# Differential attention: probabilities times values as 24 split products of 512 columns a head

## What is computed

```python
def one_block(args):                      # one block of 128 queries
    qi, pi = args
    sc = jnp.einsum('bhcqd,bhckd->bhcqk', qi, k_t).astype(jnp.float32) * scale
    ...
    p = jax.nn.softmax(sc, axis=-1)
    p_diff = p[:, :, 0] - lam * p[:, :, 1]
    return jnp.einsum('bhqk,bhkd->bhqd', p_diff.astype(v_t.dtype), v_t)
...
o = diff_attend(q, k, v, pos, lam)
o = rms_norm(o, subln_g) * (1.0 - lam_init)
return x + (o.reshape(b, s, B_WIDTH) * jax.nn.silu(gate)) @ w_out
```

## Time and profile before

| | |
|---|---|
| median of 3 runs | 3137.69 us (3137.46 to 3138.93) |
| the profiled execution: its time, its span | 3139.25 us, 3137.5 us |
| TensorE busy | 3095.8 us, 99% of the span |
| VectorE, ScalarE, GpSimd busy | 1523.7, 808.1, 2066.2 us |
| chain of work that ended last | TensorE 91%, VectorE 5% |
| TensorE clock granted, mean | 0.996 of full speed |

### The profile page before, as it was taken

The page is one execution under the profiler, slowest core; times in us unless marked ns, Lnnn a source line. Parts: engine busy times, 40 slices in busy tenths (PEclk is TensorE's granted clock), DMA queues, the critical chain, the costliest instruction groups (busy, mean ns, idle before and its releaser), DMA issues.

```text
span 3137.5 us, 59104 instructions
## 1 busy us (share of the span) xinstructions
PE 3095.8 (99%) x19614; PEld 2481.1 (79%) x19614; DVE 1523.7 (49%) x2996; ACT 808.1 (26%) x1560; POOL 2066.2 (66%) x3468
## 2 busy tenths in 40 slices
PE   8999999999999999999999999999999999999999
PEld 6777777788888787788778878888888888888777
DVE  3565555566565765611566773144234324433600
ACT  2333332243333203200355551021112112211300
POOL 7555555488787695887733456886666766666575
PEclk9999999999999999999999999999999999999999
DMA  5222221232222232233211112332222222222142
GB/s 160 62 62 62 62 61 57 62 92 80 74 80 78 70 94 78 80 94 94 74 41 33 47 40 81 94 98 81 81 74 74 80 80 74 74 81 79 54 127 87
DMA packets 461252, 239.59 MB, mean 76 GB/s; under 512 B 27917, under 2 KB 456392, under 8 KB 461128
## 3 DMA queue, kind: packets, MB, share of 16 engines
q1 hardware_dynamic: 457148, 232.14, 25.5%
q10 hardware_dynamic: 3980, 5.63, 0.5%
HBM read 233.52 MB, written 4.19 MB: 76 GB/s over the span
## 4 chain that ended last, share of the span: by engine, by line
PE 91%; DVE 5%; issue 2%; ACT 1%; DMA 0%; DVEq 0%; POOL 0%; SPq 0%; ACTq 0%; PEldq 0%; POOLq 0%
PE proj L346 25%; PE proj L347 24%; PE proj L348 24%; PE work L2598 2%; PE work L2180 2%; PE work L2173 1%; PE work L726 1%; PE work L1289 1%; PE work L346 1%; PE work L348 1%; PE work L347 1%; PE work L740 1%; PE work L1544 1%; PE work L1530 1%; DVE lat_sq L1835 0%
## 5 line engine op out<-in xcount | busy, mean ns | idle before, releaser
L318 POOL TENSOR_SCALAR w_hi<-raw_weights 128x256 fp32r<-128x256 f32 x1728 | 742.8, 456 | 1037.5 <-DMA raw_weights<-w_in 350.8
L322 POOL TENSOR_TENSOR w_lo<-raw_weights,w_hi 128x256 fp32r<-128x256 f32 x1728 | 1331.4, 801 | 0.0
L346 PE MATMUL proj<-x_hi,w_hi 128*128 128x512 f32 x2976 | 1217.7, 409 | 7.6 <-POOL w_lo L322 3.0
L347 PE MATMUL proj<-x_lo,w_hi 128*128 128x512 f32 x2976 | 1176.9, 395 | 0.0
L348 PE MATMUL proj<-x_hi,w_lo 128*128 128x512 f32 x2976 | 1176.2, 395 | 0.0
L346 PEld LDWEIGHTS proj<-x_hi,w_hi 128*128 128x128 f32 x2976 | 559.7, 188 | 152.8 <-issue 20.8
L348 PEld LDWEIGHTS proj<-x_hi,w_lo 128*128 128x128 f32 x2976 | 558.8, 188 | 136.6
L347 PEld LDWEIGHTS proj<-x_lo,w_hi 128*128 128x128 f32 x2976 | 560.3, 188 | 118.7 <-issue 2.2
L346 PE MATMUL proj<-o_hi,w_hi 128*128 128x512 f32 x256 | 103.5, 404 | 3.6 <-DVE o_lo L1175 3.2
L347 PE MATMUL proj<-o_lo,w_hi 128*128 128x512 f32 x256 | 102.0, 398 | 0.0
L348 PE MATMUL proj<-o_hi,w_lo 128*128 128x512 f32 x256 | 101.8, 398 | 0.0
(11 more groups left out here) (491 smaller groups left out, 3922.9 us busy)
## 6 DMA issues: line engine op xcount, KB each, us to landing
raw_weights<-w_in SPq DMA_DIRECT2D x260, 256.0 KB, 3.2
raw_weights<-b_w_in SPq DMA_DIRECT2D x256, 256.0 KB, 3.1
raw_weights<-a_w_in SPq DMA_DIRECT2D x100, 256.0 KB, 3.2
raw_weights<-w_out SPq DMA_DIRECT2D x64, 256.0 KB, 3.0
raw_weights<-a_w_out SPq DMA_DIRECT2D x64, 256.0 KB, 3.0
raw_weights<-b_w_out SPq DMA_DIRECT2D x64, 256.0 KB, 3.0
raw_weights<-a_w_kv_up SPq DMA_DIRECT2D x32, 256.0 KB, 2.8
mix<-x SPq DMA_DIRECT2D x4, 1024.0 KB, 8.5
```

What stands on the lines that cost most here:

```text
L318: pool.tensor_scalar(part(hi_v, s, q), part(raw_v, s, q), 1.0, 1.0, ALU.mult, ALU.mult).then_inc(hi_done, 1)
L322: pool.tensor_tensor(part(lo_v, s, q), part(raw_v, s, q), part(hi_v, s, q).bitcast(F32), ALU.subtract).then_inc(w_split, 1)
L346: pe.matmul(out, w_h, a_h, start=start, stop=False)
L347: pe.matmul(out, w_h, a_l, start=False, stop=False)
```

## The change

The product V is made once a head, for all four query blocks together, in the split form: for each half x of the value channels, four calls of `multiply` over the key blocks c, with 512 columns of queries: 2 x 4 x 3 = 24 matmuls. For this:

- the transposed probabilities of all blocks are kept, as high part (pT on ScalarE writes `d_pt_hi`) and low part, for which VectorE gets a new instruction for each block, `pl`: the transposed block in `work[2]` less its high part; the values get a low part too (`vl0`, `vl1`, VectorE);
- the room for them is taken from blocks 6 to 15 of `mix`: at the start of the stage ScalarE's queue stores these 10 blocks (2.62 MB) to `h_kept` in DRAM, and loads them back behind the last head; ScalarE and VectorE wait for the store before their first head, and VectorE waits for the load before tile 4 of the last product;
- `dpipe` has five steps instead of six; the 6 steps of fill now stand at every k, so also in front of the last transposes; V stands behind them, with 2 steps in front and 4 behind. In all there are 52 steps of fill a head instead of 50 (48 instead of 46 in the last head), and as many fewer behind it;
- T of block k-1 now waits for `pl` of block k-2, where it waited for pT of it; V waits for the last `pl`;
- ScalarE's copies `o` go: it squares V's output from PSUM directly, and VectorE multiplies it into the gates from PSUM (`og` comes before the sums; the final step is one multiplication for each half);
- in the last head VectorE cuts blocks 8 to 13 of `mix2` in pairs, behind the `pl` of blocks 1, 2 and 3 (`behind_block`).

```diff
@@ -2466,7 +2468,14 @@
         d_p = a11.over("diff_probs", d_gt_at, SEQ)
-        d_pt = a11.over("diff_probs_keys", d_gt_at + 4 * SEQ, SEQ)
+        KEPT = range(6, KB)
+        kept_at = o_start + 4 * SEQ * KEPT[0]
+        d_pt_hi, d_pt_lo = (tokens(a11.over(f"diff_probs_keys_{x}", kept_at + 4 * TB * SEQ * n, TB * SEQ, F32R)[:, :], SEQ)
+                            for n, x in enumerate(("hi", "lo")))
+        d_vt_lo = a11.over("diff_v_tok_lo", kept_at + 8 * TB * SEQ, 2 * SEQ, F32R)
+        h_kept = nc.dram_tensor("h_kept", (P, len(KEPT) * SEQ), F32).ap()
+        h_stored = sem("h_stored")
+        h_back = sem("h_back")
         d_small = a11.take("diff_small", 16 * 5)
@@ -2479,7 +2488,7 @@
         d_col = a11.take("diff_pos_col", 2 * TB)
-        dpipe = range(TB + 2)
+        dpipe = range(TB + 1)
 
@@ -2491,11 +2500,13 @@
+        DI_DVE = steps("diff_dve", "ms " + RSQRT + " nsl lq0 lq1 vl0 vl1 gate0 k0 k1 lk0 lk1 gate1 " +
+                       " ".join((f"rec{k - 1} rl{k - 1} pb{k - 1} p{k - 1} " if k else "") +
+                                (f"sca{k} mxa{k} nba{k} scb{k} mxb{k} nbb{k} " if k < TB else "") +
+                                (f"pl{k - 1}" if k else "") for k in range(TB + 1)) +
+                       " og0 oadd og1 oms " + tagged("o_") + " o0 o1")
@@ -2573,40 +2584,39 @@
                         if k == 0:
-                            need(DI_ACT, f"vt{c}")
+                            need(DI_DVE, f"vl{c}")
                             need(DI_DVE, f"lk{c}")
...
                                  True, True).then_inc(DI_PE.mark(f"S{x}{k}"), 1)
-                    yield 3
+                yield 3
                 if 1 <= k <= TB:
...
                     if k >= 2:
-                        need(DI_ACT, f"pT{k - 2}")
+                        need(DI_DVE, f"pl{k - 2}")
                     for c in range(TB):
...
                     yield 1
-                if k >= 2:
-                    need(DI_ACT, f"pT{k - 2}")
-                    if k >= 3:
-                        need(DI_ACT, f"o{k - 3}")
-                    for x in range(2):
-                        for c in range(TB):
-                            mm = pe.matmul(work[3][:, x * P:(x + 1) * P], d_vt[:, 256 * c + x * P:256 * c + (x + 1) * P],
-                                           d_pt[:, c * P:(c + 1) * P], start=(c == 0), stop=(c == TB - 1))
-                    mm.then_inc(DI_PE.mark(f"V{k - 2}"), 1)
-                    yield 1
             yield 1
-            need(DI_DVE, "oadd1")
-            token_sums(pe, work[2], d_sq[0], lambda b: b).then_inc(DI_PE.mark("osum"), 1)
+            need(DI_DVE, f"pl{TB - 1}")
+            for x in range(2):
+                for c in range(TB):
+                    vs = slice(256 * c + x * P, 256 * c + (x + 1) * P)
+                    mm = multiply(pe, work[3 - x], d_vt_hi[:, vs], d_vt_lo[:, vs], d_pt_hi[:, c], d_pt_lo[:, c],
+                                  c == 0, c == TB - 1)
+                mm.then_inc(DI_PE.mark(f"V{x}"), 1)
+            yield 2
+            need(DI_DVE, "oadd")
+            token_sums(pe, work[0], d_sq[0], lambda b: b).then_inc(DI_PE.mark("osum"), 1)
             yield behind_sums
             need(DI_DVE, "o_out_")
-            token_values(pe, work[3], d_small[:, 68:72]).then_inc(DI_PE.mark("oinv"), 1)
+            token_values(pe, work[1], d_small[:, 68:72]).then_inc(DI_PE.mark("oinv"), 1)
 
         def diff_act(act):
+            act.dma_start(h_kept, mix[:, KEPT[0] * SEQ:]).then_inc(h_stored, 16)
             pos = io["positions_2"]
@@ -2619,6 +2629,7 @@
             act.wait_ge(DP_DVE.sem, DP_DVE.after())
+            act.wait_ge(h_stored, 16)
             with act.Fori(0, B_HEADS - 1) as h:
@@ -2627,6 +2638,7 @@
             diff_heads_act(act, B_HEADS - 1, split_first, lambda k: out_split_act(act, OUT3, range(2 * k + 6, 2 * k + 8)))
+            act.dma_start(mix[:, KEPT[0] * SEQ:], h_kept).then_inc(h_back, 16)
             stage_end(act, 8, [(DI_ACT.sem, DI_ACT.after(B_HEADS)), (tile_free, T_DIFF + 8 * B_HEADS)])
@@ -2639,7 +2651,7 @@
                 need(DI_PE, f"vt{x}")
-                act.activation(tokens(d_vt[:, :], 256)[:, :, x * P:(x + 1) * P], tokens(work[x][:, :], P), ACT.Copy)\
+                act.activation(tokens(d_vt_hi[:, :], 256)[:, :, x * P:(x + 1) * P], tokens(work[x][:, :], P), ACT.Copy)\
                    .then_inc(DI_ACT.mark(f"vt{x}"), 1)
@@ -2667,19 +2679,11 @@
                     need(DI_PE, f"T{k - 1}")
-                    if k >= 2:
-                        need(DI_PE, f"V{k - 2}")
-                    act.activation(d_pt[:, :], work[2][:, :], ACT.Copy).then_inc(DI_ACT.mark(f"pT{k - 1}"), 1)
-                if k >= 2:
-                    need(DI_PE, f"V{k - 2}")
-                    act.activation(tokens(d_v[:, :], SEQ)[:, :, (k - 2) * P:(k - 1) * P], tokens(work[3][:, 0:256], P),
-                                   ACT.Copy).then_inc(DI_ACT.mark(f"o{k - 2}"), 1)
-                    if k in (3, TB + 1):
-                        x = k // TB
-                        by_half = lambda v: tokens(v, SEQ)[:, :, x * 2 * P:(x + 1) * 2 * P]
-                        act.wait_ge(DI_ACT.sem, DI_ACT.so_far(p))
-                        act.activation(by_half(d_sqs[:, 0:2 * SEQ]), by_half(d_v[:, :]), ACT.Square)\
-                           .then_inc(DI_ACT.mark(f"osq{x}"), 1)
+                    act.activation(d_pt_hi[:, :, (k - 1) * P:k * P], tokens(work[2][:, :], P), ACT.Copy)\
+                       .then_inc(DI_ACT.mark(f"pT{k - 1}"), 1)
+            for x in range(2):
+                need(DI_PE, f"V{x}")
+                act.activation(d_sq[x][:, :], work[3 - x][:, :], ACT.Square).then_inc(DI_ACT.mark(f"osq{x}"), 1)
 
@@ -2716,13 +2720,14 @@
             dve.wait_ge(NB_ACT.sem, NB_ACT.done("rinv"))
+            dve.wait_ge(h_stored, 16)
             with dve.Fori(0, B_HEADS - 1) as h:
...
             diff_heads_dve(dve, B_HEADS - 1, lambda: out_split_dve(dve, OUT3, FIRST),
-                           lambda: out_split_dve(dve, OUT3, range(*AHEAD3[0])))
+                           lambda k: out_split_dve(dve, OUT3, range(2 * k + 4, 2 * k + 6) if k >= 2 else ()))
             stage_end(dve, 8, [(DI_DVE.sem, DI_DVE.after(B_HEADS))])
 
-        def diff_heads_dve(dve, p, before_scores=lambda: None, behind_scores=lambda: None):
+        def diff_heads_dve(dve, p, before_scores=lambda: None, behind_block=lambda k: None):
             need = lambda steps, name: dve.wait_ge(steps.sem, steps.done(name, p))
@@ -2758,6 +2763,11 @@
                 low(c, dq_lo, d_q, dq_hi, "q")
+            for x in range(2):
+                need(DI_ACT, f"vt{x}")
+                by_block = lambda v: tokens(v[:, :], 256)[:, :, x * P:(x + 1) * P]
+                done(dve.tensor_tensor(by_block(d_vt_lo), tokens(work[x][:, :], P), by_block(d_vt_hi).bitcast(F32),
+                                       ALU.subtract), f"vl{x}")
             take_gate(0)
@@ -2795,21 +2805,29 @@
 
-            behind_scores()
-            for x in range(2):
-                half = slice(x * 2 * P, (x + 1) * 2 * P)
-                need(DI_ACT, f"osq{x}")
-                done(dve.tensor_tensor(d_sq[0][:, half], d_sq[0][:, half], d_sq[1][:, half], ALU.add), f"oadd{x}")
+                if k >= 1:
+                    need(DI_ACT, f"pT{k - 1}")
+                    ks = slice((k - 1) * P, k * P)
+                    done(dve.tensor_tensor(d_pt_lo[:, :, ks], tokens(work[2][:, :], P), d_pt_hi[:, :, ks].bitcast(F32),
+                                           ALU.subtract), f"pl{k - 1}")
+                behind_block(k)
+
+            def weigh(x):
+                done(dve.scalar_tensor_tensor(gate(x), gate(x), sub_gain[:, x:x + 1], work[3 - x][:, :],
+                                              ALU.mult, ALU.mult), f"og{x}")
+
+            need(DI_ACT, "osq0")
+            weigh(0)
+            need(DI_ACT, "osq1")
+            done(dve.tensor_tensor(d_sq[0][:, :], d_sq[0][:, :], d_sq[1][:, :], ALU.add), "oadd")
+            weigh(1)
             need(DI_PE, "osum")
             chain()
-            done(dve.tensor_scalar(work[2][:, 16:20], work[2][:, 0:4], 1.0 / B_V, EPS, ALU.mult, ALU.add), "oms")
-            rsqrt(dve, DI_DVE, p, work[2][:, 16:24], d_small[:, 64:68], d_small[:, 72:76], d_small[:, 68:72], "o_")
+            done(dve.tensor_scalar(work[0][:, 16:20], work[0][:, 0:4], 1.0 / B_V, EPS, ALU.mult, ALU.add), "oms")
+            rsqrt(dve, DI_DVE, p, work[0][:, 16:24], d_small[:, 64:68], d_small[:, 72:76], d_small[:, 68:72], "o_")
             need(DI_PE, "oinv")
             for x in range(2):
-                done(dve.scalar_tensor_tensor(gate(x), gate(x), sub_gain[:, x:x + 1], work[3][:, :],
-                                              ALU.mult, ALU.mult), f"og{x}")
-                chain()
-                done(dve.tensor_tensor(gate(x), gate(x), d_v[:, x * SEQ:(x + 1) * SEQ], ALU.mult), f"o{x}")
```

(17 more changed lines are left out.)

## The result

| | before | after |
|---|---|---|
| median of 12 runs each | 3139.36 us (3135.16 to 3140.11) | 3147.69 us (3144.21 to 3148.73) |
| ratio after to before | | 1.0026 [1.0018, 1.0033] |
| span of the profiled execution | 3137.5 us | 3146.6 us |
| a head, mean of heads 0 to 6 | 108.69 us | 108.64 us |
| last head, first scores to TensorE's next work | 55.66 us | 65.03 us |

The change makes the kernel 8.3 us slower, 0.3%.

A forecast was written before the change was run, and what follows sets the result against it. TensorE was taken to bound the kernel, with VectorE's attention cycle level with it. Heads 0 to 6 +14.7, last head +9.6, transfers 0: +24.3 us on 3137.69 gives 3162 us, 0.8% slower, range 3148 to 3175.

The forecast's parts named there:

- what V gives: TensorE, each head: V as 24 split matmuls takes 5.56 us instead of 7.16 in float32, gaining 1.60 us.
- T3's wait: TensorE, each of heads 0 to 6: the transposes of block 3 wait 2.88 us for VectorE's probabilities.
- pT and pl enter VectorE's chain: VectorE, blocks 1 to 3: copy and low part come after the exponentials, so the reciprocal starts 1.22 us later.
- p2 ends 7.34 + 1.22 later: VectorE, head 2: block 2's probabilities end the old 7.34 us plus 1.22 after its scaled scores start, at 2405.36.
- the same for p3 with 7.63: VectorE, head 2: block 3's probabilities end 7.63 + 1.22 us after its scaled scores start, at 2414.25.
- net +2.1 us a head: Heads 0 to 6: 3.7 us of waits at the transposes less 1.6 gained on V; times 7, +14.7 us.
- Rival 2: Attention chain late, but little: p and neighbours shorten as GpSimd has less to do; stands for 3137 to 3144, chance 0.08.
- The last head: Last head: longer VectorE chain with its cuts, then fill, V and sums; TensorE's next work at 2987.3 against 2977.71, +9.6 us.
- store and load: Moving 2.62 MB to DRAM and back around the stage: 11.2 us each, covered by slack, so 0 added.
- Rival 4: The transfers hold back the weight loads: +2 to +5 us on the forecast, 3164 to 3180, chance 0.12.
- Rival 1: The attention's chain hides pT and pl, only TensorE's work counts: 3137.7 - 12.8 = 3125, chance 0.06.
- its lower bound: Low end of the range: cycles faster by 0.6 us each give 3152, taken down to 3148.

The follow-up runs named there:

- experiment 2: Low parts of the attention stage's weights left out on GpSimd, in both kernels: 3140.11 us on the kernel before, 3136.72 on the changed one.
- experiment 1: Changed kernel with 8 steps of fill instead of 6 in front of the last transposes of heads 0 to 6: 3138.23 us, ratio to before 0.9996.
- experiment 3: Kernel before with only the store and load back of blocks 6 to 15 and their waits added: 3139.53 us, ratio 1.0.
- Experiment 7: Changed kernel with 8 steps of fill before heads 0 to 6's last transposes and both last-head cuts moved (VectorE's before pl, ScalarE's behind pT): 3130.5 us.

## Why the prediction was right or wrong

**Right: TensorE bounds, and what V gives.** 1.60 us a head were computed; the pair of experiment 2 gives 1.75, experiment 1 gives 1.43 (108.69 - 107.26). Of the 0.3 us between the two, 0.2 is what is left of T3's wait in experiment 1; without it, its heads take 107.04, as those of the changed kernel do without what T3's wait costs (107.05). That is a gain of 1.64. The last 0.1 stays open.

**Right: pT and pl enter VectorE's chain.** 1.22 us a block forecast, 1.12 measured, with pl at the 0.69 of the earlier trace rows. It doesn't contend, as argued. p1 of head 2 ended 18.06 us behind the first scores, 18.14 by the prediction's sum.

**Wrong: the step "p2 ends 7.34 + 1.22 later", and the same for p3 with 7.63.** The prediction carried the cycle lengths of before over to a chain that starts at another time. Both held an R of 2.85 us. The term is mis-sized by 0.90 in block 2 (R 1.94) and by 1.18 in block 3 (R 1.67). By the prediction's own working p3 ends 35.63 us behind the first scores; measured are 33.59, and the two terms explain 2.08 of these 2.04. T2 thus waits for nothing instead of 0.83, and as T2 then no longer holds TensorE up, T3's wait should come down to 2.88 - 2.04 + 0.83 = 1.67; it is 1.56 in head 2 and 1.44 in the mean. From start to start it costs 1.59 against a gain of 1.64, so net +2.1 us a head becomes nothing: 14.7 us of the forecast are -0.3. The earlier trace rows had shown the price (p 1016 ns against 748), and the text cited the rule on GpSimd; both were used only for whether pl would suffer, and not for what a later chain would shed of its own contention. The product with lambda, 0.13 and 0.39 of the two terms, was in no row. The bound for it was missing: the trace of before has both instructions free, too (R is 1.67 to 2.9 over its 32 blocks).

**Rival 2 was the mechanism, with the wrong chance.** It said that p and its neighbours would come down, gave 3147 for 0.8 us less a cycle, and then kept only 3137 to 3144 for itself with a chance of 0.08. Its reason, that GpSimd has less to do while TensorE waits, is not what the runs show: GpSimd does the same work in heads 0 to 6 (894 instructions both times, 494 us against 507), and R moved into its pauses. The 3147 is also partly luck: it had the last head 4 us shorter, which it wasn't, and the seven heads 3.5 longer than they were.

**The last head: the sum right, its terms not.** 65.25 us were forecast (2987.3 - 2922.05), 65.03 measured. The chain was shorter than forecast: p3 ended 41.6 us behind the first scores instead of 43.95, R being 1.7 to 1.8 there. The way from T3 to `oinv` was longer, 2984.12 - 2964.50 = 19.6 instead of 17.6: T3 itself took 1.05 for 0.60, and the nine matmuls from 2967.57 took 3.91 instead of 2.1 us, both at half clock. The two misses cancel. That the fill would also wait for block 10 (3.10 us), and that the clock would fall with it, stood nowhere in the prediction.

**Right: store and load.** 9.4 us against 11.2 estimated. Rival 4's mechanism is real (GpSimd idle for 7.82 us) and costs nothing; experiment 3 has the ratio at 1.0 [0.999, 1.0009].

**Rival 1** (all hidden, 3125) is wrong as the kernel stands: the chain was not short enough for T3. Experiment 7, at 3130.5, comes nearest to it.

**The range** ended at 3148, since its lower bound took 0.6 us off a cycle where 0.9 to 1.2 were to be had. The bound would have had to be R at its shortest in the trace, 1.67, in both blocks: 1.2 less each, which the rival's own sum puts below 3141.

## What to carry to other kernels

When a chain of VectorE shifts against GpSimd's work, its instructions change their length: bound each by its shortest and longest occurrence in the trace of before, not by the one at the same place. A chain that is delayed can slide out from under the contention, and one that is made earlier can slide back in, so that an edit of a microsecond moves the end by a few tenths in either direction. And before a product is given up as too dear, put independent work in front of its consumer: here 1.4 us of fill turned 8 us slower into no difference, and with two splits moved into 9 us faster.
